# Two blocks of a transformer on one core: matmuls whose result nobody reads, placed in TensorE's waits

## What is computed

```python
def first_block(x, ...):
    hn = rms_norm(x, norm1_g)
    proj = hn @ w_in                       # q, k, v of two attentions
    out_a = global_gqa_attention(qa, ka, va)
    out_b = dilated_mixture_attention(rms_norm(qb, ...), rms_norm(kb, ...), vb)
    x = x + mixed @ w_out                  # mixed: both outputs, normed
    x = x + conv_ffn(rms_norm(x, norm2_g), w_up, conv_w, conv_b, w_down)

def second_block(x, c, ctx, ...):
    for l in range(2):                     # 256 tokens of x and 256 of ctx
        h_l = modulate(xl, norm_mix_g[l], mod_l[0], mod_l[1])   # rmsnorm, scale, shift
        o_l, o_c = hybrid_mixer(...)       # differential attention and a chunked
                                           # state-space scan, gated and projected
        xl = xl + mod_l[2] * o_l
        xl = xl + mod_l[5] * sq_relu_mlp(modulate(xl, norm_mlp_g[l], ...), w_mlp1[l], w_mlp2[l])
        # the same for xc (ctx) in layer 0 only
    return rmsnorm(xl, final_norm_g)
```

## Time and profile before

| | |
|---|---|
| median of 3 runs | 2636.26 us (2635.76 to 2637.47) |
| span of the profiled execution | 2637.3 us |
| PE busy | 2498.4 us (95%) |
| DVE busy | 1216.2 us (46%) |
| ACT busy | 1127.8 us (43%) |
| POOL busy | 1493.0 us (57%) |
| DMA | 313.00 MB, mean 119 GB/s |

### The profile page before, as it was taken

One profiled execution on the slowest core, in us unless ns is written; L12 is line 12 of the kernel. 1 busy time (PEld: TensorE's weight loads), 2 busy tenths in 40 slices (PEclk: granted clock), 3 DMA queues, 4 the chain that ended last, 5 costly groups with the idle time before them and its releaser, 6 DMA issues.

```text
span 2637.3 us, 39465 instructions
## 1 busy us (share of the span) xinstructions
PE 2498.4 (95%) x15396; PEld 2178.1 (83%) x15396; DVE 1216.2 (46%) x2583; ACT 1127.8 (43%) x2371; POOL 1493.0 (57%) x1318
## 2 busy tenths in 40 slices
PE   7999999998899999999999999989989999888998
PEld 6679997885688888888878787888868888788998
DVE  3545502226737888773342112122464888743210
ACT  2345533115526776773032002042364667544532
POOL 1018765760354554544965788764234666656875
PEclk9999999999899999999989999989999999999999
DMA  7566453227532222215323333333444322264564
GB/s 205 176 189 178 126 154 106 82 95 256 180 96 65 78 56 67 72 49 158 98 64 96 96 96 96 90 102 96 160 148 120 88 80 80 81 175 136 185 160 112
DMA packets 388967, 313.00 MB, mean 119 GB/s; under 512 B 12576, under 2 KB 374082, under 8 KB 387778
## 3 DMA queue, kind: packets, MB, share of 16 engines
q1 hardware_dynamic: 385874, 297.75, 38.4%
q10 hardware_dynamic: 2352, 12.59, 1.2%
q0 software_dynamic: 576, 0.43, 0.2%
HBM read 303.40 MB, written 7.34 MB: 118 GB/s over the span
## 4 chain that ended last, share of the span: by engine, by line
PE 73%; POOL 9%; DVE 9%; issue 5%; ACT 2%; DMA 2%; POOLq 1%; SPq 0%; DVEq 0%; ACTq 0%
PE PS L696 35%; PE PS L1073 10%; POOL rounded L2647 9%; PE PS L754 5%; PE PS L1080 3%; PE PS L719 3%; DVE mid_a L2390 2%; PE PS L1201 2%; PE PS L1114 2%; PE PS L654 2%; PE PS L1123 2%; PE PS L992 1%; PE PS L1004 1%; PE PS L904 1%; DVE mid_v L2444 1%
## 5 line engine op out<-in xcount | busy, mean ns | idle before, releaser
L2647 POOL TENSOR_TENSOR rounded<-ring,rounded 128x512 fp32r<-128x512 f32 (+1 forms) x872 | 1112.0, 1307 | 775.0 <-ACT rounded L1326 446.2
L696 PE MATMUL PS<-rounded 128*128 128x256 f32 (+1 forms) x6864 | 1149.9, 330 | 26.2 <-DVE rounded L2584 8.1
L696 PEld LDWEIGHTS PS<-rounded 128*128 128x128 f32 x6864 | 1028.4, 192 | 142.5 <-issue 10.5
L2670 POOL TENSOR_TENSOR rounded<-ring,constants 128x512 fp32r<-128x512 f32 x216 | 229.3, 1092 | 274.8 <-PE PS L696 142.6
L1073 PE MATMUL PS<-rounded 128*128 128x512 f32 (+1 forms) x1536 | 347.2, 383 | 11.6 <-POOLq L2617 6.5
L1073 PEld LDWEIGHTS PS<-rounded 128*128 128x128 f32 x1536 | 277.9, 190 | 67.5 <-POOLq L2617 6.8
L1326 ACT ACTIVATE rounded<-ring 128x2048 fp32r<-128x2048 f32 (+1 forms) x99 | 180.0, 1822 | 157.9 <-DMA ring<-in_w_mlp_dram 59.4
L2390 DVE SCALAR_TENSOR_TENSOR mid_a<-PS,V,mid_a 128x510 f32<-128x510 f32 (+3 forms) x256 | 182.2, 714 | 28.7 <-ACT mid_a L1655 21.2
L1693 ACT ACTIVATE rounded<-constants,big 128x128 fp32r<-128x128 f32 x384 | 150.2, 391 | 0.0
L1693 ACT ACTIVATE rounded<-constants,mid_v 128x128 fp32r<-128x128 f32 x384 | 150.1, 391 | 0.0
L1080 PE MATMUL PS<-rounded 128*128 128x256 f32 x1152 | 147.8, 286 | 0.0
(11 more groups left out here) (261 smaller groups left out, 3061.4 us busy)
## 6 DMA issues: line engine op xcount, KB each, us to landing
ring<-in_w_mlp_dram SPq DMA_DIRECT2D x64, 1024.0 KB, 5.5
ring<-in_w_in_dram SPq DMA_DIRECT2D x56, 1024.0 KB, 5.4
ring<-in_ada_w_dram SPq DMA_DIRECT2D x48, 1024.0 KB, 5.3
ring<-in_w_in_dram SPq DMA_DIRECT2D x81, 512.0 KB, 4.1
ring<-in_w_up_dram SPq DMA_DIRECT2D x44, 512.0 KB, 5.2
ring<-in_w_ssd_o_dram SPq DMA_DIRECT2D x16, 1024.0 KB, 5.9
ring<-in_w_out_dram SPq DMA_DIRECT2D x12, 1024.0 KB, 5.0
ring<-in_w_down_dram SPq DMA_DIRECT2D x16, 704.0 KB, 4.7
```

Source lines behind the costliest of these rows:

```text
L696: mm = pe.matmul(PS[:, b, 0:cols], w[:, k, m * P:(m + 1) * P], x(half * kt + k), start=(half == 0 and k == 0 and n_pass == 0), stop=(half ...
L2647: ins = pool.tensor_tensor(lo[:, r], raw[:, r], hi[:, r], ALU.subtract)
L2670: ins = pool.tensor_tensor(hi[:, r], raw[:, r], ones[:, 0:1].broadcast_to([P, 512]), ALU.mult)
```

## The change

The change adds a helper, `fill`, that issues matmuls of the all-ones constant with 256 columns of other constants, with nothing waited for and nobody told. Their results are overwritten by the next matmul into that bank. No instruction is removed and no other engine's program changes. There are 76 of them:

- setup: 2 behind the transposes, 4 behind the spread;
- six norms: ahead of the sums of squares, ahead of the spread, and behind it: (1, 1, 3), (1, 1, 7), (3, 1, 6), (3, 1, 7), (1, 1, 3), (1, 1, 3) in order of time;
- 3 behind the first two score units of each layer;
- 3 behind the transposes of the attention's output in each layer;
- 4 (layer 0) and 9 (layer 1) between the signal and the wait of the fence in `stage`.

```diff
--- before.py
+++ after.py
@@ -605,9 +605,10 @@
             c = Counts(pe)
             slab, tile, bank4, fences = [0], [0], [0], [0]
 
-            def stage():
+            def stage(fills):
 
                 pe.drain().then_inc(*c.made(fence))
+                fill(fills, 0)
                 fences[0] += 1
                 pe.wait_ge(fence, 4 * fences[0])
 
@@ -763,13 +764,20 @@
                        + [(q, 16) for q in slot_loaded] + [(split_ready, SLOTS)] * (parts is not None))
                 ring_end(freed)
 
-            def mean_square(k, sq, cols):
-
+            def fill(n, bank):
+
+                for _ in range(n):
+                    pe.matmul(PS[:, bank, 0:SEQ], ones, K[:, 0:SEQ], start=True, stop=True)
+
+            def mean_square(k, sq, cols, fills=None):
+
+                if fills:
+                    fill(fills[0], 5)
                 pe.wait_ge(*c.need(squares))
                 mm = sums_by_token(k, sq, k == 0, cols // P)
                 if k == KT - 1:
                     mm.then_inc(*c.made(mean_sq))
-                    spread_rms(cols // P)
+                    spread_rms(cols // P, fills)
 
             def sums_by_token(k, sq, first, n_tok=TT):
 
@@ -778,15 +786,20 @@
                                    stop=(k == KT - 1 and t == n_tok - 1))
                 return mm
 
-            def spread_rms(n_tok=TT):
-
+            def spread_rms(n_tok=TT, fills=None):
+
+                if fills:
+                    fill(fills[1], 5)
                 for t in range(n_tok):
                     pe.wait_ge(*c.need(rms_diag))
                     mm = pe.matmul(PS[:, 4, t * P:(t + 1) * P], ones, y_diag[:, t, :], start=True, stop=True)
                 mm.then_inc(*c.made(rms_spread))
-
-            def mean_of_sums(sq):
-
+                if fills:
+                    fill(fills[2], tile[0] % 4)
+
+            def mean_of_sums(sq, fills):
+
+                fill(fills[0], 5)
                 pe.wait_ge(*c.need(sq_summed))
                 sums_by_token(0, sq, True)
                 c.skip(squares, KT - 2)
@@ -794,7 +807,7 @@
                     pe.wait_ge(*c.need(squares))
                     mm = sums_by_token(k, sq, False)
                 mm.then_inc(*c.made(mean_sq))
-                spread_rms()
+                spread_rms(TT, fills)
 
             def one_behind(sq, cols, halves=1, first=1):
 
@@ -834,10 +847,12 @@
             pe.wait_ge(gain_loaded, 16)
             turn([vstage[0:KT, 0, :]])
             turn_end()
+            fill(2, 3)
             for t in range(LT):
                 pe.wait_ge(*c.need(rms_diag))
                 mm = pe.matmul(PS[:, 4, t * P:(t + 1) * P], ones, x_diag[:, t, :], start=True, stop=True)
             mm.then_inc(*c.made(rms_spread))
+            fill(4, 3)
             lat = lambda k: hT[:, k, 0:SEQ]
             def head_squares(n):
 
@@ -947,7 +962,7 @@
             c.skip(turned_freed, -4)
             to_features(4, lambda k: mix1[:, k, :], SEQ, dve_freed, after=one_behind(hT, SEQ),
                         first_rows=lambda: pe.wait_ge(*c.need(turned_freed)))
-            mean_square(KT - 1, hT, SEQ)
+            mean_square(KT - 1, hT, SEQ, (1, 1, 3))
             c.skip(scaled, KT)
             to_features(FFT, lambda k: hm_hi[1][:, k, :], SEQ, dve_freed, loads=2, body=FFT, row_ready=rows(), aside=2,
                         rest=lambda k: hm_lo[:, k, 0:SEQ], hi_at=up_at, lo_at=up_rest_at)
@@ -958,9 +973,9 @@
 
             for l in range(LAYERS):
                 if l == 0:
-                    mean_square(KT - 1, hT, T)
+                    mean_square(KT - 1, hT, T, (1, 1, 7))
                 else:
-                    mean_of_sums(hT)
+                    mean_of_sums(hT, (3, 1, 7))
                 c.skip(scaled, 2 * KT)
                 n_half = 2 if l == 0 else 1
                 q_cols = n_half * SEQ
@@ -1009,6 +1024,7 @@
                 mods = mods_of[1 + l]
                 scores2(0)
                 scores2(1)
+                fill(3, 7)
                 for u in range(n_u + 1):
                     if u + 2 < n_u:
                         scores2(u + 2)
@@ -1026,6 +1042,7 @@
                 turn_begin()
                 for f in range(KT):
                     turn([o2[:, t, f * P:(f + 1) * P] for t in range(n_tok)])
+                fill(3, tile[0] % 4)
                 turn_end()
 
                 def decay_sums(n):
@@ -1041,7 +1058,7 @@
 
                 to_features(4, lambda k: att_hi[l][:, k, :], q_cols, dve_freed, rest=lambda k: att_lo[l][:, k, :],
                             hi_at=mix_at[l], after=decay_sums)
-                stage()
+                stage(4 if l == 0 else 9)
 
 
                 ny = len(y_chunks(l))
@@ -1255,9 +1272,9 @@
                 to_features(4, lambda k: merged_hi[l][:, k, :], q_cols, dve_freed, rest=lambda k: merged_lo[l][:, k, :],
                             hi_at=gate_at[l], row_ready=rows(), aside=2, after=one_behind(out_sq[l], q_cols, first=2) if l else None)
                 if l == 0:
-                    mean_of_sums(out_sq[l])
+                    mean_of_sums(out_sq[l], (3, 1, 6))
                 else:
-                    mean_square(KT - 1, out_sq[l], q_cols)
+                    mean_square(KT - 1, out_sq[l], q_cols, (1, 1, 3))
                 c.skip(scaled, n_half * KT)
                 first_row = dict(row_ready=rows(n_half), first_at=first_mlp[l], aside=4 if l == 0 else 2)
                 h_parts = dict(rest=lambda k: hm_lo[:, k, 0:q_cols], hi_at=mlp_at[l])
```

## The result

The changed kernel takes 2619.33 us (median of 4 runs, 2617.60 to 2620.88), the kernel before beside it 2636.86 us (4 runs, 2635.76 to 2640.28). The ratio is 0.9932 with a 95% interval of 0.9919 to 0.9945: faster by 0.68%, some 18 us. The forecast was 2615.6 us in a range of 2604 to 2628 us. The change does what its mechanism says, at nearly the size of the sum; two of the eleven terms came out with the wrong sign, one for the worse (the norm ahead of layer 0) and one for the better (behind the second turned attention).

What follows compares the result with a forecast made beforehand. PE, holding 73% of the chain, was taken as the bound, at half clock behind its waits; eleven terms summed to 20.7 us saved, 2636.3 - 20.7 = 2615.6 us, range 2604 to 2628 us.

Steps and rivals of the forecast that it cites:

- the norm ahead of layer 0: Product behind this norm back at full clock, though perhaps not for all of it: 2.4 us saved.
- behind the second turned attention: Layer 1's attention output: fillers outlast the 1.1 us wait, a loss of 0.5 us.
- the rival by which only part of the clock is held: Norms' stretches stay at half clock, the other places are held: 9.9 us saved, 2626 us, chance 0.20.
- The rival on the slow side: Fillers don't lift the clock, take 0.86 us each at half clock and outlast their waits: 2656 us, chance 0.05.
- The projection's rival: The 64-column projection, without fillers, also keeps its clock in layer 0: 5.2 us more saved, 2610 us, chance 0.20.
- The setup's 2.9 us: First products of the setup at full clock, fillers done before the transfer that ends the wait: 2.9 us saved.
- The starts of the attentions: Full clock at the start of both attentions, 1.0 us saved at each, 2.0 us together.
- the norm ahead of layer 1: At full clock PE would wait for VectorE's rows, so only 0.8 us saved.
- The MLP norm of layer 0: Half-clock piece stays in the 24 sums, the product's first part gains full clock: 2.2 us saved of 4.9.
- The late start of the sums: At the two norms with `mean_of_sums`, three fillers held back by a wait make the sums 0.6 us late.
- The fences: Scan's first products behind both fences at full clock: 3.8 us saved.
- the rule weighed there: Skill's rule that transposes don't engage full clock: fillers behind turned attention would cost 0.8 us, sum 18.2 us; set aside.

Runs made afterwards that it cites:

- one_column: Changed kernel with its 76 fillers in place but one column each instead of 256: 2636.45 us, 0.9998 of the kernel before.
- norms_only: Changed kernel with only the 45 fillers of the six norms kept: 2626.96 us, 0.9963 of the kernel before.
- no_layer0_norm: Changed kernel without the nine fillers of the norm ahead of layer 0: 2620.19 us, 0.9943 of the kernel before.
- early: Changed kernel with each norm's first fillers issued ahead of the wait for the last emptied bank, counts unchanged: 2620.73 us, 0.9941 of the kernel before.
- psum_diag: Changed kernel with VectorE's norm diagonals made from an identity that a filler leaves in PSUM, instead of SBUF: 2619.19 us, 0.9945 of the kernel before.
- both: `more2` with the `psum_diag` edit added: 2617.44 us, 0.9930 of the kernel before.
- rest_only: Changed kernel with only the 31 fillers of setup, attentions, turned attentions and fences kept: 2625.69 us, 0.9961 of the kernel before.
- more2: Changed kernel plus the places added in `more`, norms' first fillers unmoved, ten before the first turned attention issued ahead of their wait: 2614.38 us, 0.9921 of before.
- more: `early` plus fillers at up-projection ends, before the projection behind the scan, ten before the first turned attention, twelve inside the second: 2620.34 us, 0.9936 of before.

## Why the prediction was right, and where it was not

**The mechanism held.** The clock over products behind a wait was low because PE had waited, and plain matmuls on constants hold it. `one_column` is the test: same instructions, no columns, no gain. That the constants are nearly all zeros does not matter, and the rival by which only part of the clock is held (2626 us) is refuted; `norms_only` shows the norms paying on their own. The rival on the slow side needed the fillers at 0.43 us a record; in the first norm six take 1.46 us, 0.24 us each.

**The step that failed: the norm ahead of layer 0**, taken at -2.4 and measured at +1.3. The product's half of it is right (-1.6). Ahead of it VectorE's diagonals took 3.6 us longer, and the product began 2.9 us later. The prediction priced each wait as PE's alone and moved all earlier savings through it at no cost; it did not ask what GpSimd's weight split would be doing when PE arrives 6.0 us earlier. What is shown: the fillers of the place are not the cause (`no_layer0_norm`), and over the traces two groups stand apart. In five (the changed kernel, its repetition, `no_layer0_norm`, `early`, `one_column`) GpSimd's eight instructions run without a pause and the four diagonals take 4.3 to 4.7 us. In the other nine, before among them, GpSimd pauses after four and they take 0.9 to 1.5 us. `norms_only` has the changed kernel's fillers at this norm and the pause:

```profile
394.81 4.99 POOL L2660 TENSOR_TENSOR rounded<-ring,rounded 128x512 fp32r<-128x512 f32 x4 [3.24 <-ACT rounded L1324]
...
399.21 1.26 DVE L1957 TENSOR_SCALAR constants<-constants,stat 128x128 f32<-128x128 f32 x4
...
400.84 4.97 POOL L2660 TENSOR_TENSOR rounded<-ring,rounded 128x512 fp32r<-128x512 f32 x4 [1.04 <-ACT rounded L1324]
```

Its way to the product is +0.3 where the changed kernel's is +2.9, so the missing pause costs about 2.6 us here; over all traces the way is 2.9 to 4.2 us longer than before's without the pause and between 0.8 us shorter and 1.8 us longer with it. That VectorE is shut out by GpSimd is shown by the ends of the diagonals, which follow GpSimd's one by one when the identity is read from SBUF, and don't when it is read from PSUM (`psum_diag`, `both`). What is not shown is the time of the whole place with the PSUM diagonals and no pause. What remains of the miss, 1.0 us (-1.4 in `norms_only` for -2.4), goes with the way to the product, part of which ran at half clock there (399.9 to 403.3 us); no run isolates it.

**The projection's rival** (2610 us) had its event and not its price. The fall did move away: the 64 records of layer 0 took 7.36 us, as in layer 1. It gave 0.6 us and not 5.2, as the rows of the changed kernel show:

```profile
694.19 7.36 PE L755 MATMUL PS<-ring,hT 128*128 128x64 f32 x64 [0.44 <-DVE mid_o L2314]
...
697.33 8.62 DVE L2339 TENSOR_TENSOR mid_o<-mid_o,stat 128x1024 f32<-128x1024 f32 x4
...
706.53 5.89 PE L836 MATMUL PS<-constants,mid_o 128*128 128x128 f32 x32 [4.98 <-DVE big L2343]
```

PE now waits 4.98 us for VectorE, whose scaling takes 8.62 us and reads nothing of the projection. In before the same work lay hidden behind PE's slow 12.58 us. The rival's price took PE's time alone and didn't ask what paces the stretch next.

**The smaller terms.** First norm (2.5), final norm (1.4) and the turned attention of layer 0 (2.0 for 1.7) are as worked out, and `one_column` has none of them. The setup's 2.9 us are in the products in both profiles of the change, but the prediction's "the fillers are done before" is wrong: the first product began 0.7 and 1.0 us later than in before, and against the kernels with nothing to hold the clock there only 0.3 to 1.3 us are the fillers'. The starts of the attentions (3.0 for 2.0), the fence of layer 0 and the norm ahead of layer 1 (1.9 for 0.8) can't be called right, since `one_column` has 2.8, 1.5 and 1.5 us at them. Behind the second turned attention a loss of 0.5 was forecast and 0.9 us were gained (1.0 in `rest_only`, 0.1 or less either way in `one_column` and `norms_only`): the prediction counted there what the fillers outlast, and nothing for the clock behind them. The MLP norm of layer 0 was cut to 2.2 because the run of 24 sums would fall to half clock whatever stands around it; with three fillers ahead of it the run kept the full clock, 2.73 us for 4.45:

```profile
1350.54 1.56 PE L770 MATMUL PS<-constants 128*128 128x256 f32 x6 [0.97 <-DVE xT L2572]
1351.94 2.73 PE L785 MATMUL PS<-constants,big 128*128 128x1 f32 x24
...
1355.56 1.98 PE L795 MATMUL PS<-constants 128*128 128x128 f32 x8 [0.35 <-DVE constants L1961]
```

The clock fell only behind them, at L795 (1.98 us for eight). The step "the fillers do not change the run itself" is wrong, and the size came near since the later fall took back part. The late start of the sums was 0.7 us as forecast (0.6). The fences gave 2.9 for 3.8 us, since the wait at the second is still 0.87 us and its first product came 0.8 us late. Errors of both signs at these places nearly cancel the failed term, and before's one trace had half-clock pieces that the change gets credit for. That the total of 20.7 came out so close to 20.6 is luck in this measure; the medians lie 17.5 us apart.

**What stays open** is small differences. The kernel before ranged from 2628.90 to 2643.97 us over 28 runs of one batch, and in the traces single half-clock stretches of 1.5 us each come and go at untouched places. Medians of five or six runs don't resolve edits of 1 to 3 us, and so `early`, `more2`, `psum_diag` and `both` have no verdict against the changed kernel.

## What to carry to other kernels

Where the granted clock is half behind a wait and PE is on the chain, fill that wait with matmuls of many columns, as long as the wait and no longer: 33 us of them (76 at 0.43 us) bought 18 us here, one-column ones nothing, twice as many cost 24 us more than the change. See what the first filler itself waits for: behind a wait instruction it starts with the releaser and not when PE falls idle, and stands in the way (the ten in `more`, the two in the setup). Ahead of the wait takes the lateness away (`early`), but it is not a safe place either: the ten in `more2` cost as much in the execution in which the work before them had filled the wait. And price each gain against the next engine in that stretch, and ask of every later meeting point what has run into what when PE arrives early: the failed term and the projection's rival were both wrong in that way, by 2.6 us and by 4.6 us.

## What the runs showed of the hardware that was not expected

- VectorE's one-source instruction of 128x128 float32 in SBUF takes 0.22 us with GpSimd pausing (0.87 us for four) and one GpSimd instruction each, 1.2 us, while GpSimd runs 1.23 us instructions back to back (4.51 us for four), each ending 0.08 us behind a GpSimd instruction. Reading its source from PSUM it took 0.28 us (1.13 us for four in `both`), three of the four inside one GpSimd instruction.
- The granted clock came up from half to full inside a run of transposes, the 32 at L836 behind PE's wait of 4.98 us, with nothing else on PE. These are two stretches within that run in the changed kernel:

```profile
706.50:710.50 4.00, 3.97 (x19) 3.97 (x20) 2.61 (x4) 2.32 (x4) 4.00 (x5) 0.50 0.00 0
710.60:712.20 1.60, 1.59 (x15) 1.35 (x14) 1.50 (x3) 1.60 (x4) 1.52 (x2) 1.00 0.00 0
```

  The prediction kept its term of 1.7 us behind them against the rule weighed there, and the place gave 2.0 us.

- The 24 one-column matmuls of the sums took 2.73 us behind three fillers (granted clock 1.00 over them) and 4.25 us behind an idle PE, where before they had taken 4.45 us. That is not so everywhere: at the norm ahead of layer 1 they took 3.34 us behind an idle PE in before, and 3.60 us behind three fillers in `early`.
